# Gate statistics as columns: 20 transposes inside a query tile in place of 60 narrow products, tile 4's convolution ahead of a split

## What is computed

```python
def mlstm_prep(p, conv_w, b_gates, with_q):
    k = to_heads(silu(dw_conv(p[..., OFF_ML_K:OFF_ML_V], conv_w[:, ML_WIDTH:])), N_ML_HEADS)
    q = to_heads(silu(dw_conv(p[..., OFF_ML_Q:OFF_ML_K], conv_w[:, :ML_WIDTH])), N_ML_HEADS)
    v = to_heads(p[..., OFF_ML_V:OFF_ML_O], N_ML_HEADS)
    g = (p[..., OFF_ML_G:OFF_GLA_Q] + b_gates).astype(f32)      # 4 heads x (input, forget) x 2 directions
    ...
    fwd = (q, k, v, g[0], log_sigmoid(g[1])); bwd = (q, k, v, g[2], log_sigmoid(g[3]))
```

## Time and profile before

| | |
|---|---|
| median of three runs | 1340.05 us |
| span of the profiled execution | 1339.0 us |
| mean granted clock of TensorE | 0.978 |
| TensorE busy | 1265.4 us, 95% |
| weight loads busy | 1100.0 us, 82% |
| VectorE busy | 950.9 us, 71% |
| ScalarE busy | 776.2 us, 58% |
| chain that ended last | TensorE 82%, VectorE 9%, ScalarE 4%, DMA 3% |

### The profile page before, as it was taken

How to read it: one execution, slowest core, us unless ns; L and a number is a source line. 1 busy time by engine, 2 the same in 40 slices (tenths; PEclk the granted TensorE clock), 3 DMA queues, 4 the chain that set the end, 5 groups by cost and what they waited for, 6 DMA issues and landing times.

```text
span 1339.0 us, 18966 instructions
## 1 busy us (share of the span) xinstructions
PE 1265.4 (95%) x7151; PEld 1100.0 (82%) x7151; DVE 950.9 (71%) x1104; ACT 776.2 (58%) x911; POOL 119.1 (9%) x127
## 2 busy tenths in 40 slices
PE   6899999999999999999997599999999999999994
PEld 4888788898988999878886588888888888888883
DVE  5857431278666862584546988888888898888887
ACT  6643321374425454782333277777777777777785
POOL 1100000010000000041000111111111000111034
PEclk9999989999999999999998799999999999999997
DMA  9851160143454411304226599999999999999995
GB/s 376 280 119 34 62 189 0 48 127 111 158 221 172 174 65 33 142 22 184 79 80 230 228 362 352 406 400 405 397 396 396 396 391 399 397 396 396 395 312 211
DMA packets 77659, 319.35 MB, mean 239 GB/s; under 512 B 6568, under 2 KB 31176, under 8 KB 47832
## 3 DMA queue, kind: packets, MB, share of 16 engines
q1 hardware_dynamic: 70336, 290.14, 55.2%
q0 software_dynamic: 7264, 28.40, 8.5%
HBM read 291.15 MB, written 35.75 MB: 244 GB/s over the span
## 4 chain that ended last, share of the span: by engine, by line
PE 82%; DVE 9%; ACT 4%; DMA 3%; issue 1%; SPq 0%; POOLq 0%; POOL 0%; DVEq 0%; ACTq 0%
PE psum L2656 37%; PE psum L2263 7%; PE psum L2592 7%; PE psum L2321 3%; PE psum L2322 3%; PE psum L2323 3%; PE psum L2352 1%; PE psum L2353 1%; PE psum L2354 1%; DMA ada_raw<-w_ada_units 1%; PE psum L2164 1%; PE psum L2404 1%; PE psum L2679 1%; PE psum L2405 1%; PE psum L2673 1%
## 5 line engine op out<-in xcount | busy, mean ns | idle before, releaser
L2026 DVE TENSOR_TENSOR e_lo<-e_raw,e_hi 128x2048 fp32r<-128x2048 f32 x192 | 432.8, 2287 | 43.5 <-ACT e_hi L1331 43.5
L1331 ACT ACTIVATE e_hi<-e_raw 128x2048 fp32r<-128x2048 f32 x192 | 365.8, 1916 | 82.9 <-PE psum L2656 81.8
L2656 PE MATMUL psum<-e_hi,xt_hi 128*128 128x512 f32 x496 | 153.3, 390 | 0.1
L2656 PE MATMUL psum<-e_lo,xt_hi 128*128 128x512 f32 x496 | 152.9, 389 | 0.0
L2656 PE MATMUL psum<-e_hi,xt_lo 128*128 128x512 f32 x496 | 152.8, 389 | 0.0
L2656 PEld LDWEIGHTS psum<-e_hi,xt_lo 128*128 128x128 f32 x496 | 93.1, 188 | 19.6
L2656 PEld LDWEIGHTS psum<-e_lo,xt_hi 128*128 128x128 f32 x496 | 93.1, 188 | 19.6
L2656 PEld LDWEIGHTS psum<-e_hi,xt_hi 128*128 128x128 f32 x496 | 92.8, 188 | 19.8 <-DVE xt_lo L2030 0.5
L2321 PE MATMUL psum<-w_hi,h_hi 128*128 128x256 f32 x352 | 101.4, 288 | 0.0
L2322 PE MATMUL psum<-w_hi,h_lo 128*128 128x256 f32 x352 | 100.3, 285 | 0.0
L2323 PE MATMUL psum<-w_lo,h_hi 128*128 128x256 f32 x352 | 100.2, 285 | 0.0
(11 more groups left out here) (436 smaller groups left out, 2435.5 us busy)
## 6 DMA issues: line engine op xcount, KB each, us to landing
e_raw<-w_e_units SPq DMA_DIRECT2D x192, 1024.0 KB, 7.5
ada_x<-w_ada_units SPq DMA_DIRECT2D x16, 1024.0 KB, 4.8
raw<-w_in_units SPq DMA_DIRECT2D x13, 1024.0 KB, 6.8
ada_raw<-w_ada_units SPq DMA_DIRECT2D x8, 1024.0 KB, 21.9
bc<-rows_dram SPq DMA_DIRECT2D x16, 512.0 KB, 3.8
xs<-x SPq DMA_DIRECT2D x4, 1024.0 KB, 10.4
acc_dram<-zero_r SPq DMA_DIRECT2D x1, 4096.0 KB, 19.8
wo_raw<-w_out SPq DMA_DIRECT2D x4, 1024.0 KB, 6.0
```

Of the source, the lines that this page charges most:

```text
L1331: act.activation(e_hi[u % EH][:], e_raw[u][:], ACT.Copy).then_inc(e_hi_ok, 1)
L2026: dve.tensor_tensor(e_lo[u][:], e_raw[u][:], e_hi[u % EH][:], ALU.subtract).then_inc(e_lo_ok, 1)
L2656: m = pe.matmul(o[:, BANK * b:BANK * (b + 1)], x[:, k, :], w[:, D * j + BANK * b:D * j + BANK * (b + 1)], start=a, stop=z)
```

## The change

The three statistics are turned by transposes. `row_a` now holds two of them: its first 64 partitions the log term, its last 64 the exponential of `row_f` (ACT writes it there, 64 partitions in place of 128). Ten transposes turn 128 x 128 chunks of `row_a` into banks 2, 3 and 6, ten more turn 36 x 128 chunks of `row_m` into bank 7. They are issued from inside unit 11's second tile (tile 7), four behind each of its first five steps of k. DVE copies the columns out in eight small copies, which now stand between `split_lo(13)` and `split_lo(14)`.

`conv_first(4)` moves ahead of the exponentials on ACT, `conv_taps(4)` ahead of `split_lo(11)` on DVE.

Two waits of TensorE change. In `t_unit` the wait on `g_free` stays only for the second tile of the pair (tile 3). Ahead of the v stage it waits for `conv_free` 7 instead of 8, and 8 moves behind the second v tile.

```diff
+        STAT_CHUNKS = (4, 4, 2)
+        def stat_af(g):
+            b = (2, 3, 6)[g]
+            return psum[:, b * BANK:(b + 1) * BANK].rearrange("p (c n) -> p c n", n=P)
+        stat_m = psum[:, 7 * BANK:7 * BANK + 36 * TA].rearrange("p (c n) -> p c n", n=36)
...
             conv_first(3, 1, 1, True)
+            conv_first(4, 1, 2, True)
             act.wait_ge(row_dve, 1)
             act.activation(rows32[:, 1, :], rows32[:, 1, :], ACT.Exp).then_inc(row_act, 1)
-            act.activation(row_f[:], row_f[:], ACT.Exp).then_inc(row_act, 1)
+            act.activation(row_a[64:P, :], row_f[0:64, :], ACT.Exp).then_inc(row_act, 1)
             act.activation(row_m[:], row_m[:], ACT.Exp, scale=-1.0, bias=ln_hd[:, 0:1]).then_inc(row_act, 1)
             split_hi(11)
             conv_silu(2, 1, 0)
             conv_silu(3, 1, 1)
-            conv_first(4, 1, 2, True)
...
+            conv_taps(4, 1, 2)
             split_lo(11)
-            conv_taps(4, 1, 2)
...
             split_lo(13)
+            dve.wait_ge(stat_mm, 1)
+            for g, n in enumerate(STAT_CHUNKS):
+                for q in range(2):
+                    v = stat_af(g)[:, 0:n, 64 * q:64 * q + 64].rearrange("p c (d x) -> p c d x", d=2)
+                    dve.tensor_copy(cst[:, q, 4 * g:4 * g + n, :].rearrange("p c (d h) -> p c d h", d=2), v[:, :, :, 0:NH])
+            for d in range(2):
+                i = dve.tensor_copy(cst[:, 2, :, NH * d:NH * d + NH], stat_m[:, :, 32 * d:32 * d + NH])
+            i.then_inc(stat_ready, 1)
             split_lo(14)
             conv_taps(8, 0, 2)
             conv_taps(9, 0, 3)
-            dve.wait_ge(stat_mm, 1)
-            dve.tensor_copy(cst[:].rearrange("p q c s -> p (q c s)"), psum[:, 7 * BANK:7 * BANK + 3 * TA * 2 * NH]).then_inc(stat_ready, 1)
...
-            def t_unit(n, i0, has_ctx, free):
+            def t_unit(n, i0, has_ctx, free, behind=None):
                 unit_ready(n)
                 for j in range(2):
-                    if free is not None:
+                    if free is conv_free or free is g_free and j:
                         pe.wait_ge(free, i0 + j - 1 - (2 if free is conv_free else 0))
-                    last = t_tile(i0 + j, n, j, has_ctx)
+                    last = t_tile(i0 + j, n, j, has_ctx, behind if j else None)
...
-            t_unit(11, 6, False, conv_free)
+            def stat_rows(k):
+                if k == 0:
+                    pe.wait_ge(row_act, 4)
+                if k >= TA // 2:
+                    return
+                for c in (2 * k, 2 * k + 1):
+                    pe.transpose(stat_af(c // 4)[:, c % 4, :], row_a[:, P * c:P * (c + 1)], ident[:])
+                    i = pe.transpose(stat_m[:, c, :], row_m[0:36, P * c:P * (c + 1)], ident[0:36, 0:36])
+                if k == TA // 2 - 1:
+                    i.then_inc(stat_mm, 1)
+            t_unit(11, 6, False, conv_free, stat_rows)
             t_unit(12, 8, False, conv_free)
-            pe.wait_ge(row_act, 4)
-            for q, src in enumerate((row_a, row_f, row_m)):
-                for c in range(TA):
-                    o = 7 * BANK + (q * TA + c) * 2 * NH
-                    last = pe.matmul(psum[:, o:o + 2 * NH], src[:, P * c:P * (c + 1)], sel_s[:], start=True, stop=True)
-            last.then_inc(stat_mm, 1)
...
-            pe.wait_ge(conv_free, 8)
+            pe.wait_ge(conv_free, 7)
             pe.wait_ge(stat_ready, 1)
...
                 if p == 1:
+                    pe.wait_ge(conv_free, 8)
                     pe.wait_ge(conv_act, 8)
```

## The result

The changed kernel takes 1330.38 us (median; 1327.59 to 1331.14), the kernel before 1341.1 us on the same chip (1339.75 to 1343.67): a ratio of 0.9916, interval 0.9897 to 0.9934. That is 10.7 us gained where 17.6 were forecast; 1322.5 us was predicted, and the range ended at 1328. The profiled execution took 1329.71 us with a span of 1328.0.

A forecast was written before the change was run, and what follows sets the result against it. TensorE's instruction stream, busy 95% of the span, was taken as the critical path almost everywhere. 1.40 + 3.13 + 1.73 - 2.20 + 10.54 + 2.98 = 17.6 us saved, span 1339.0 to 1321.4, time 1322.5 us, range 1319.5 to 1328.

The forecast's parts named there:

- the transposes: Twenty transposes inside tile 7 at 0.11 us each: 2.2 us added, bounds 2.1 to 4.4 us.
- Of the start-to-start gap 136.48 to 139.61 all 3.13 us go: Ahead of tile 6: with tile 4's convolution moved earlier, TensorE's wait vanishes, saving 3.13 us.
- 1.73 us of half clock: In tile 6: half clock goes with the wait, so 12.61 us becomes 10.88 us, saving 1.73 us.
- the first two parts: Tile 2 without its wait and tile 4's convolution moved ahead: 1.40, 3.13 and 1.73 us saved.
- the 60 products: Narrow products after tile 9: removal saves 10.54 us, and 2.98 us of half clock at the start of v.
- Tile 2 starts at the gate tile's end: Tile 2 starts at 78.29 instead of 80.10, 1.81 us earlier, of which 1.40 us is kept.
- v is not held: V stage starts at 180.8 without waiting for unit 14 or the taps, with at least 1.4 us of room.
- the moved copy: ScalarE's copy of tile 4, ahead of the exponentials: hidden, with 1.6 us to spare.
- A: Rival: the clock falls behind the transposes in tile 7, giving 1324.2 to 1327.7 us; chance 0.10.
- B: Rival: slower, the clock staying down from the first burst to tile 9's end, giving 1350 us; chance 0.02.
- D: Rival: nearly no gain, within 0.2% (2.7 us), v held at its old 195.4 by the data; chance 0.02.
- C: Rival: part of the gain is given back later, by shifted waits and clock dips to 600 us; 1320.5 to 1329; chance 0.12.

The follow-up runs named there:

- grouped: Changed kernel with the row_a transposes in the first four bursts and all ten row_m transposes in the fifth: 1326.28 us (one run).
- full: Changed kernel with all twenty transposes over 128 partitions, order kept: 1326.9 us, ratio 0.989 to the kernel before.
- late_products: Kernel before with tile 2's wait removed and tile 4's convolution moved, but the 60 narrow products still after tile 9: 1337.18 us, ratio 0.9967.
- full_fill: Changed kernel with all transposes over 128 partitions, plus 20 unused products in TensorE's wait at 44 to 47 us: 1325.34 us, ratio 0.988.
- after_third: Changed kernel unedited, run once more on another chip for a third trace: 1328.97 us, ratio 0.9916.
- before_again: Kernel before unedited, run once more for a second trace: 1341.61 us, ratio 1.0007.
- again: Changed kernel unedited, run once more for a second trace: 1329.69 us, ratio 0.9916.

## Why the prediction was wrong

**The step that failed in size: the transposes.** "Nearest row: 8 transposes between v products take 0.88 us ... 20 x 0.11 = 2.2 us added." They take 4.8. The row that I scaled from holds transposes of one size only, and the second bound, from 8-column products, was one size too. The upper bound of 4.4 us did not even hold the value. Ordered by size the term is nearly right as it stood (2.2 in grouped, 2.35 in full).

**The step that failed in basis: one execution taken for the kernel.** "Of the start-to-start gap 136.48 to 139.61 all 3.13 us go", and 1.73 us of half clock with it. "Its instruction stream is the critical path" holds for shares over the span, but ahead of tile 6 the chain ran through the load of unit 10, ScalarE's exponentials and VectorE's taps of tile 4 (14.17 us from the exponential to tile 6 in each trace of the old kernel that waits there), and TensorE's wait at tile 6 was only what its early arrival left over. Its 2.97 us, with 1.73 us of half clock behind them, were this execution's; the same kernel had 1.24 us and no half clock in the next execution profiled, in which that load took 4.8 us and not 6.6. So 3.13 + 1.73 is what one kind of execution gives, and not the middle of all. The sum mended with what the runs showed is 17.6 - 2.5 (transposes) - 3.4 (131.03 - 127.64) = 11.7 us, near the measured 10.7 to 11. The first correction is shown by experiments. The second rests on two single traces, so its size for the median is an estimate, and 3.4 is all that lies between them; late_products, where the first two parts gain 4.1 us instead of 6.3, points the same way with 2.2. With 2.2 the sum is 12.9; that what is left is the 1.6 us by which the 60 products differ between traces is possible, not shown.

**In the profiled pair** the gate tile's end adds 2.70 us, of which 0.41 come back because the stall at tile 4 doesn't occur (unit 10's load, on which the taps of tile 2 hang, took 4.8 us instead of 6.6), and the second half-clock spell at 412 to 424 most of the last 2.0. Neither is the change's doing as far as these runs tell. The path that the sum took to the median, "1.05 above the profiled span", mixed two executions; it should have been 1.7. The prediction also places the first dips of the clock "in slices 5 and 6"; the line in the earlier trace rows shows one in slice 6 only, and the half clock at 142 is known from the earlier trace rows. Nothing in the sum rests on it.

**What was right.** Tile 2 starts at the gate tile's end; tile 6 has no wait and no half clock; the wait for `row_act` inside tile 7 is empty; v is not held by unit 14 or by the taps and takes 10.89 us from its start to the context transposes instead of 13.91 (209.32 - 195.41), 3.0 us less as in the sum; the clock stays full beside the transposes. VectorE's eight copies take 0.94 us, six of them 0.64 and two 0.30 (rows below), where 1.6 were allowed. In the changed kernel the exponentials are not delayed by the moved copy, but only a tenth of a microsecond was left.

```profile
173.08 0.64 DVE L1624 COPY cst<-psum 128x32 f32<-128x32 f32 x6
173.64 0.30 DVE L1626 COPY cst<-psum 128x40 f32<-128x40 f32 x2
```

**The rivals.** A, B and D did not occur. C did in part. The case that did occur, transposes at twice their price with a gain from a wait that is only partly there, was among none of them: the measured 1330.38 lies above C's far end, 1329, and the range, which ended at 1328, left it out.

## What to carry to other kernels

Price an instruction by a row with the same neighbours, not only the same kind: TensorE work of another partition count put between full-size work cost some 0.13 us here at each change of size, so keep sizes together, or make the small ones full-size where the output has room. Before a wait of one engine goes into a sum, follow the chain of whoever ends it back to its start: if it starts from the same event as the waiting engine's own stretch, the wait is a difference of two paths, varies from execution to execution (here with the time of one load), and swallows early arrivals, so take a second trace of the old kernel for it. And where a removed wait is followed by half clock, look whether other executions show it at all.

## What the runs showed of the hardware

A change between 128-partition and 36-partition transposes costs some 0.13 us, while ten 36-partition transposes in a row take 0.74 us. The same 1 MB load took 4.7 to 5.0 us in nine traces and 6.5 to 7.8 in the eight in which it was issued earlier, with more of a 2 MB copy still under way beside it (the cause is argued, not tested). Twenty transposes in bursts among dense products leave the clock at full speed (1.00 from 148 to 164 us). The wait of TensorE of 2.9 to 3.2 us that ends at 46 to 49 us stands in all traces but full_fill's; half clock follows it in nine (the changed kernel, after_third and before_again among them; 1.3 to 2.7 us lost up to the next wait) and full clock in seven (before and again among them). So here a wait of that length was followed by the dip in some executions and not in others, and a price for it needs more than one trace.
